# A hybrid decoder trunk on one core: landing ring of 12 units, ring of split weights of four halves

## The reference, cut to what matters

```python
for l in range(DEPTH):                       # DEPTH = 2
    mod = (silu(c) @ w_ada[l] + b_ada[l])    # shift1, scale1, gate1, shift2, scale2, gate2
    h = rmsnorm(x, norm1_g[l]) * (1.0 + scale1) + shift1
    u = h @ w_in[l]                          # 1024 x 3072: u_b, u_c, u_h, u_q, u_k, u_v
    y_conv = u_b * conv3(u_c * u_h)          # causal, three taps
    q, k = rope(rmsnorm(heads(u_q))), rope(rmsnorm(heads(u_k)))
    y_att = softmax(q @ k.T / 8, causal) @ v # 8 heads of 64; one block of 256 keys
    y_mix = concat(rmsnorm(y_conv), rmsnorm(y_att))
    x = x + gate1 * (y_mix @ w_out[l])
    h2 = rmsnorm(x, norm2_g[l]) * (1.0 + scale2) + shift2
    x = x + gate2 * hier_moe(h2)             # 16 SwiGLU experts of 256, two per token in one of 4 groups
```

## Time and profile before

| | before |
|---|---|
| time, median of 3 runs | 645.54 us (645.4 to 645.75) |
| the profiled execution | 644.83 us, span 642.9 us |
| TensorE matmul busy | 558.6 us (87%) |
| VectorE busy | 287.0 us (45%) |
| ScalarE busy | 217.4 us (34%) |
| loaded | 189.76 MB, mean 295 GB/s |
| mean granted TensorE clock | 0.948 of 2.4 GHz |

### The profile page before, as it was taken

The page is one execution under the profiler, slowest core; times in us unless marked ns, Lnnn a source line. Parts: engine busy times, 40 slices in busy tenths (PEclk is TensorE's granted clock), DMA queues, the critical chain, the costliest instruction groups (busy, mean ns, idle before and its releaser), DMA issues.

```text
span 642.9 us, 7867 instructions
## 1 busy us (share of the span) xinstructions
PE 558.6 (87%) x3148; PEld 352.8 (55%) x3148; DVE 287.0 (45%) x492; ACT 217.4 (34%) x376; POOL 13.7 (2%) x64
## 2 busy tenths in 40 slices
PE   2749999869798999999958999986976799999993
PEld 0338899445665544444426899844564654454431
DVE  4165790885247122222278496286426512222233
ACT  2064543532124522222145544264105333223120
POOL 7100000000000000000000000000000000000000
PEclk9969999988898999999998999997978699999998
DMA  8999943691299999999999737097059069999941
GB/s 266 370 389 388 402 174 131 267 409 44 73 423 408 394 364 408 413 415 412 408 387 356 250 132 261 4 405 311 1 197 389 3 259 380 417 414 414 414 187 68
DMA packets 48623, 189.76 MB, mean 295 GB/s; under 512 B 4346, under 2 KB 4426, under 8 KB 40388
## 3 DMA queue, kind: packets, MB, share of 16 engines
q1 hardware_dynamic: 47264, 185.62, 74.0%
q10 hardware_dynamic: 900, 3.23, 1.3%
q0 software_dynamic: 416, 0.32, 0.5%
HBM read 188.10 MB, written 1.05 MB: 294 GB/s over the span
## 4 chain that ended last, share of the span: by engine, by line
PE 77%; DVE 11%; ACT 5%; DMA 4%; issue 1%; SPq 1%; DVEq 0%; ACTq 0%
PE ps L1399 17%; PE ps L1213 11%; PE ps L1201 11%; PE ps L1425 9%; PE ps L1304 6%; PE ps L1379 6%; PE ps L1439 5%; DMA raw<-in_w_ada_dram 4%; PE ps L1121 4%; DVE wlo L702 2%; PE ps L1144 2%; PE ps L1294 1%; ACT work L478 1%; DVE stat L864 1%; DVE work L859 1%
## 5 line engine op out<-in xcount | busy, mean ns | idle before, releaser
L702 DVE TENSOR_TENSOR wlo<-raw,whi 128x1024 fp32r<-128x1024 f32 x64 | 74.9, 1220 | 14.0 <-ACT whi L443 13.8
L443 ACT ACTIVATE whi<-raw 128x1024 fp32r<-128x1024 f32 x64 | 64.6, 1059 | 26.0 <-PE ps L1201 10.5
L1121 PE MATMUL ps<-raw,c_rep 128*32 128x512 f32 x384 | 50.2, 660 | 17.4 <-DMA raw<-in_w_ada_dram 17.3
L1399 PE MATMUL ps<-raw,qkT 128*64 128x512 f32 x256 | 58.3, 597 | 1.6 <-ACT work L653 1.6
L1425 PE MATMUL ps<-raw,work 128*64 128x512 f32 x256 | 58.0, 598 | 0.0
L1399 PE MATMUL ps<-raw,cbc 128*64 128x512 f32 x256 | 57.2, 594 | 0.0
L1065 DVE SCALAR_TENSOR_TENSOR work<-ps,cw,work 128x256 f32<-128x256 f32 x16 | 11.0, 685 | 102.7 <-ACT work L647 102.7
L1213 PE MATMUL ps<-act_hi,whi 128*128 128x256 f32 x192 | 54.5, 284 | 0.0
L1213 PE MATMUL ps<-act_hi,wlo 128*128 128x256 f32 x192 | 54.3, 283 | 0.0
L1213 PE MATMUL ps<-act_lo,whi 128*128 128x256 f32 x192 | 54.3, 283 | 0.0
L1054 DVE TENSOR_TENSOR v_sb<-ps,gates 128x512 f32<-128x512 f32 x32 | 22.1, 691 | 64.6 <-PE ps L1425 64.6
(11 more groups left out here) (215 smaller groups left out, 850.2 us busy)
## 6 DMA issues: line engine op xcount, KB each, us to landing
raw<-in_w_ada_dram SPq DMA_DIRECT2D x48, 1024.0 KB, 9.8
raw<-in_w_gate_dram SPq DMA_DIRECT2D x64, 512.0 KB, 7.5
raw<-in_w_up_dram SPq DMA_DIRECT2D x64, 512.0 KB, 8.9
raw<-in_w_down_dram SPq DMA_DIRECT2D x32, 1024.0 KB, 10.9
raw<-in_w_in_dram SPq DMA_DIRECT2D x24, 1024.0 KB, 14.6
raw<-in_w_out_dram SPq DMA_DIRECT2D x8, 1024.0 KB, 5.4
gates<-in_b_ada_dram ACTq DMA_DIRECT2D x4, 512.0 KB, 6.5
res<-in_x_dram ACTq DMA_DIRECT2D x1, 1024.0 KB, 5.1
```

Source lines behind the costliest of these rows:

```text
L443: act.activation(whi[:, slot(n), :], raw[:, r, (i % 2) * 1024:(i % 2 + 1) * 1024], ACT.Copy).then_inc(hi_done, 1)
L702: dve.tensor_tensor(wlo[:, slot(n), :], raw[:, ring_slot[("w", l, i // 2)], (i % 2) * 1024:(i % 2 + 1) * 1024], whi[:, slot(n), :].bitcast ...
L1121: ins = pe.matmul(ps[32 * i:32 * i + 32, 6, :], c_rep[:, k, :], raw[:, ring_slot[unit], i * 512:(i + 1) * 512], start=(k == 0), stop=(k == ...
L1399: ins = pe.matmul(ps[i * SLOTS:(i + 1) * SLOTS, 0, :], hg[p // 2 % 2][:, k, c0:c0 + SLOTS], ws[i][:, :, kk, :], start=(k == 0), stop=(k == ...
```

## The change

The landing ring becomes 12 units, the rings of split halves 4 (a half may be split when the half four before it has been used), and the mapping of halves to slots is moved so that half 0 of layer 1 falls on the one free slot. Each split call in the lists of ScalarE and VectorE is moved one unit later. At the end of layer 0 one half of layer 1 is split instead of three; the others follow after the norm. Unit 14, which was split during attention, is split after the conv norm's root on ScalarE and after the last head's output on VectorE.

```diff
-RING = 6
-RAW = 10
+RING = 4
+RAW = 12
...
         def slot(n):
-            return (n + 1) % RING
+            return (n + 3) % RING
...
# ScalarE
                 if l == 0:
-                    for u in range(3):
+                    for u in range(2):
                         split(l, u)
                 else:
...
-                    for i in (3, 4, 5):
+                    for i in (1, 2, 3):
                         split_half(l, i)
                 gate_biases(l)
-                split(l, 3)
+                split(l, 2)
...
                 qk_out(0)
+                split(l, 3)
                 split(l, 4)
+                qk_out(1)
                 split(l, 5)
-                qk_out(1)
                 split(l, 6)
-                split(l, 7)
                 act.wait_ge(qk_sum, l + 1)
...
+                split(l, 7)
                 split(l, 8)
-                split(l, 9)
                 act.wait_ge(unit_used, n0 + 16)
...
+                split(l, 9)
                 split(l, 10)
-                split(l, 11)
                 act.wait_ge(unit_used, n0 + 20)
...
+                split(l, 11)
                 for w in range(2):
                     act.wait_ge(qkT_done, 2 * l + w + 1)
...
                 exps(3)
-                split(l, 14)
                 pT_out(3)
...
+                split(l, 14)
                 act.wait_ge(yatt_sum, l + 1)
...
                 if l + 1 < L:
-                    for i in range(3):
-                        split_half(l + 1, i)
+                    split_half(l + 1, 0)
...
# VectorE
-                for i in range(0 if l == 0 else 3, 6):
+                for i in range(0 if l == 0 else 1, 4):
                     split_half(l, i)
...
+                split(l, 2)
                 split(l, 3)
                 split(l, 4)
-                split(l, 5)
                 dve.wait_ge(proj_evac, 5 * l + 2)
...
                                   AX.X, ALU.add).then_inc(qk_sum, 1)
+                split(l, 5)
                 split(l, 6)
-                split(l, 7)
                 dve.wait_ge(qk_root, l + 1)
...
-                    split(l, 8 + t)
+                    split(l, 7 + t)
+                split(l, 9)
                 split(l, 10)
                 split(l, 11)
...
                 heads_out(2)
-                split(l, 14)
                 gate_add(l, 1)
...
                 heads_out(3)
+                split(l, 14)
...
                 if l + 1 < L:
-                    for i in range(3):
-                        split_half(l + 1, i)
+                    split_half(l + 1, 0)
```

## The result

The changed kernel takes **651.4 us** (median of 5 runs, 650.09 to 653.61) against 645.4 us (5 runs, 644.34 to 645.75): 6.0 us slower, ratio 1.0103 with a 95% interval of 1.0076 to 1.0129. (Every ratio here is estimated from all the runs of both kernels, and so it is not quite the quotient of the two medians.) Forecast were 650.6 us and +5.1. The profiled execution took 653.4 us (span 651.6, mean granted clock 0.937); three of the five runs had 0.943 and took 650.09 to 651.4. So some 2 us of what the profile shows are not in the median; they go with the lower clock.

A forecast was written before the change was run, and what follows sets the result against it. TensorE was taken as the bound, running projections and experts almost without waits after the first modulation loads. Terms 4.6 - 1.9 + 1.45 + 1.0 = +5.1 us on the median of 645.54 gave 650.6 us, own range 649 to 652.5.

The forecast's parts named there:

- q/k/v, +1.9 and +0.4 a layer: Projection stage: TensorE stalls 1.9 us at half 10 and 0.4 us at half 16, +4.6 us for two layers.
- Transition, -1.9: End of layer 0's experts: with one half split instead of three, the residual addition and everything behind come 1.9 us earlier.
- Half 1, +1.45: Start of layer 1: half 1, now split behind the norm's parts, comes late and stalls TensorE 1.45 us.
- Unit 14, 0: Attention and output projection: the later split stays hidden, slack 0.6 and 1.8 us, cost 0, at most 2 us a layer.
- Landing ring, 0: Weight loads: going from 10 to 12 units changes nothing, at most 1.4 us gained at the start.
- Clock, +1.0, behind the stalls: Projection stage: one of the two 1.9 us stalls lowers TensorE's clock, costing 1.0 us, between 0 and 2.0.
- The row of 1.84 us: Profile before: idle time before 145.01 us, followed by granted clock 0.56; taken as nearest to the 1.9 us stalls.
- a clock row that differs in more than one place a layer: Sign, in the changed profile, that would show the forecast wrong; it charged a clock fall behind one of two stalls.
- No fall with the stalls: Rival: the projection stalls come but the clock does not fall, 649.6 us; chance 0.22.
- Projection late: Rival: output projection's slack is used up, modulation row or attention root handed over late, 652.6 to 654.6 us; chance 0.10.
- no stalls: Rival: the projection stalls don't show and only the transition acts, 645.1 us; chance 0.10.
- The clock on the other side: Rival: gate and norm matmuls in both layers escape the low clock, saving 6.2 us in all, 643.4 us; chance 0.08.

The follow-up runs named there:

- e1: Kernel before, with only the splits of units 3 to 11 moved one place later and the old rings kept: 653.51 us, ratio 1.0112.
- e5: Changed kernel, with the low part of half 10 made on VectorE between the squares and their sum: 654.56 us, ratio 1.012.
- e3: Kernel before, with unit 14 alone split late and its halves waiting as in a ring of four: 645.89 us, ratio 0.9987.
- e4: Changed kernel, with the landing ring back at 10 units: 652.58 us, ratio 1.0093.
- e7: Kernel before, with 32 further matmuls nobody reads after the last scatter of layer 0: 649.17 us, ratio 1.0063.
- e9: Kernel before, with one half ahead at the transition, half 1 behind the second norm bank, 10 unread matmuls behind TensorE's branch: 649.87 us, ratio 1.006.

## Why the prediction was right

- **q/k/v, +1.9 and +0.4 a layer.** Right in place and size: half 10 lags by 1.88, half 16 by 0.44. With 0.2 us of small hand-overs a layer that is 2.5 where 2.3 were forecast. e1 shows that order alone does it, e5 that the two waits are one lateness (2.45 us in sum in both kernels).
- **Transition, -1.9.** Right: -1.83. **Half 1, +1.45.** This term failed in its mechanism: the wait did not come. Its low part was as late as worked out, but half 0 ran at 1.2 GHz and ended later still; the loss there is 1.85 us. Net 0 instead of -0.45. I had priced the clock only behind the new waits and not behind the idle time that this edit shortens.
- **Unit 14, 0.** Right: slack 0.8 us, e3 at 0.9987. **Landing ring, 0.** Right: e4.
- **Clock, +1.0, behind the stalls.** This step failed in its mechanism too: none of the six waits of 1.7 us at half 10 (changed kernel, e1, e4) was followed by a fall; the halves behind it ran at 0.23 us a matmul, and the granted clock has no low stretch there. The changed kernel, from the start of the projections at full clock to the gate matmuls, layer 0 and layer 1, with both waits inside each window:

```profile
58.00:143.00 85.00, 76.63 (x549) 64.03 (x548) 58.63 (x76) 38.96 (x67) 0.00 (x0) 1.00 0.76 292
352.00:447.00 95.00, 86.63 (x593) 72.29 (x593) 64.17 (x88) 42.47 (x71) 0.00 (x0) 1.00 0.62 228
```

  The row of 1.84 us was a bad neighbour: it stands in a stage where TensorE is idle again and again, which may be what sets it apart, though no run tests that. The Trainium skill (TensorE: Matmul & The Clock Gate, section HAM oscillation) says that it is idle gaps clearly longer than these that throw the clock back. The waits of 1.71 us agree with it, and the fall behind the 1.84 us row remains against it. The clock did cost something, in the attention stages, 1.7 to 1.9 us each in the profile, over half 0 of layer 1, and at the start. By the prediction's own sign, a clock row that differs in more than one place a layer, it was wrong about the clock. If the waits are as long in the runs without a profile, they and the transition make +5.0, and the median's other 1.0 us is what is left for the clock; that agrees with the 1.0 I charged by luck.
- **Rivals.** "No fall with the stalls" was true of its mechanism and 1.8 us low in its time. "Projection late" and "no stalls" are refuted by the rows above. "The clock on the other side" came out with the other sign: the attention stages lost time to the clock instead of winning some.

## What to carry to other kernels

When a ring becomes shallower, look for the longest block of other work in the list of the engine that fills it, and ask which item is due at its end: here 4.7 us of squares and sums, which begin 1.3 us into the 5.4 us that TensorE takes for the unit before. Mend a lateness for the whole stretch or it moves to the next item. A microsecond won ahead of an idle time isn't won until the clock behind it has been read; and where variants differ by under 1%, compare their mean granted clocks before explaining their times.

## What the runs showed of the hardware

- The same attention stage ran in 42.9, 44.75 and 46.8 us at granted clocks of 0.92, 0.89 and 0.82, with the same waits in it. In its 76 runs beside the experiments the kernel before took 644.0 to 647.0 us at a mean of 0.948 (42 runs), 646.1 to 648.5 at 0.945 (14) and 647.2 to 648.6 at 0.940 or 0.941 (12).
- With only a branch on a value loaded from memory between two matmuls in TensorE's list, 3.3 us of idle time lay between them when 7.4 us of extra matmuls stood right ahead of it (e7), and 6.0 us when they didn't (e9); before, it lay in idle time.
- Six idle times of 1.7 us between dense matmuls (changed kernel, e1, e4) left the clock at 2.4 GHz, and so did the two of 1.5 us in e5; one of 1.84 us in a sparse stage, with others around it, did not.
